# The experts' weights read in neighbouring rows, and the recurrence keys' norms computed in 32-column tiles

## The reference

```python
kk = heads(k * k_k)                      # [L, 8 heads, 64]
kk = kk * lax.rsqrt(jnp.maximum(jnp.sum(kk * kk, axis=-1, keepdims=True), 1e-24))
...
g = jax.nn.sigmoid(hg) @ gate_g2         # [L, 96] @ [96, 512]
```

```python
xs = h[idx]                                               # [128, 1024] per expert
hid = silu(xs @ w_gate[e]) * (xs @ w_up[e])               # w_gate, w_up: [1024, 512]
y = (hid @ w_down[e]) * g                                 # w_down: [512, 1024], added into the output rows
```

## Time and profile before

| | us |
|---|---|
| median of three runs | 4886.32 |
| lowest and highest | 4883.38, 4889.38 |
| the profiled execution | 4879.66 |
| its span on the core | 4877.9 |
| recurrence keys, first scaling to last multiplication | 755.4 to 794.8 |
| experts of layer 0, first to last product of hidden values (L3919) | 3386.6 to 3761.0 |
| experts of layer 1, likewise | 4537.8 to 4821.7 |

### The profile page before, as it was taken

The page is one execution under the profiler, slowest core; times in us unless marked ns, Lnnn a source line. Parts: engine busy times, 40 slices in busy tenths (PEclk is TensorE's granted clock), DMA queues, the critical chain, the costliest instruction groups (busy, mean ns, idle before and its releaser), DMA issues. The chain is left out here.

```text
span 4877.9 us, 89645 instructions
## 1 busy us (share of the span) xinstructions
PE 4396.5 (90%) x39314; PEld 3460.2 (71%) x39314; DVE 2089.0 (43%) x3007; ACT 1367.6 (28%) x2034; POOL 1051.8 (22%) x756
## 2 busy tenths in 40 slices
PE   6998996999998989999989889997999688996897
PEld 3878885999994478888867657674776574774776
DVE  2026544444443134323422144416666414434886
ACT  2114202222222020000012133314665212322775
POOL 2310122444432123333322010021221111000111
PEclk9999997999998999999999889998999889998998
DMA  7310110000006311111121000027998210002998
GB/s 277 100 48 7 44 27 27 4 4 4 3 4 271 116 47 46 49 48 47 47 104 40 26 23 1 14 89 293 301 304 251 83 33 23 1 27 108 337 375 287
DMA packets 322596, 480.33 MB, mean 98 GB/s; under 512 B 43665, under 2 KB 201322, under 8 KB 313042
## 3 DMA queue, kind: packets, MB, share of 16 engines
q1 hardware_dynamic: 301778, 399.61, 23.9%
q0 software_dynamic: 17024, 63.11, 4.6%
q10 hardware_dynamic: 3456, 12.58, 0.7%
HBM read 420.71 MB, written 54.53 MB: 97 GB/s over the span
## 5 line engine op out<-in xcount | busy, mean ns | idle before, releaser
L3895 DVE TENSOR_TENSOR l_experts_lo<-l_raw_room,l_experts_hi 128x1024 fp32r<-128x1024 f32 x256 | 300.2, 1220 | 61.1 <-ACT l_experts_hi L3828 60.6
L3828 ACT ACTIVATE l_experts_hi<-l_raw_room 128x1024 fp32r<-128x1024 f32 x256 | 256.1, 1058 | 66.4 <-PEq L69 32.1
L180 PE MATMUL mlp_ps<-h_hi,mlp_w_hi 128*128 128x512 f32 x512 | 201.0, 393 | 9.0 <-DVE h_lo L590 9.0
L180 PE MATMUL mlp_ps<-h_lo,mlp_w_hi 128*128 128x512 f32 x512 | 200.3, 391 | 0.0
L180 PE MATMUL mlp_ps<-h_hi,mlp_w_lo 128*128 128x512 f32 x512 | 200.2, 391 | 0.0
L1788 POOL TENSOR_TENSOR rec_lv<-rec_ab,rec_masks 128x512 f32<-128x512 f32 x120 | 145.0, 1225 | 243.5 <-DVE rec_ab L1705 157.0
L1724 DVE TENSOR_TENSOR rec_x<-rec_x,rec_all_ps 128x1024 f32<-128x1024 f32 (+1 forms) x100 | 111.4, 1114 | 194.2 <-PE rec_all_ps L1506 194.2
L2369 ACT ACTIVATE mlp_hid_hi<-mlp_pos 128x1024 f32 x32 | 34.0, 1062 | 569.3 <-DVE mlp_pos L2379 569.3
L180 PE MATMUL mlp_ps<-mlp_hid_hi,mlp_w_hi 128*128 128x512 f32 x448 | 174.3, 389 | 0.0
L180 PE MATMUL mlp_ps<-mlp_hid_lo,mlp_w_hi 128*128 128x512 f32 x448 | 174.3, 389 | 0.0
L180 PE MATMUL mlp_ps<-mlp_hid_hi,mlp_w_lo 128*128 128x512 f32 x448 | 174.3, 389 | 0.0
(11 more groups left out here) (716 smaller groups left out, 11507.8 us busy)
## 6 DMA issues: line engine op xcount, KB each, us to landing
l_raw_room<-in_w_gate_dram SPq DMA_DIRECT2D x128, 512.0 KB, 6.6
l_raw_room<-in_w_up_dram SPq DMA_DIRECT2D x128, 512.0 KB, 7.9
l_experts_raw_down<-in_w_down_dram SPq DMA_DIRECT2D x64, 1024.0 KB, 7.5
rec_out_w_ada<-in_w_ada_dram SPq DMA_DIRECT2D x24, 1024.0 KB, 12.3
mlp_w<-in_w_mlp_up_dram SPq DMA_DIRECT2D x32, 512.0 KB, 3.9
mlp_w<-in_w_mlp_down_dram SPq DMA_DIRECT2D x32, 512.0 KB, 4.0
l_choose_w_ada<-in_w_ada_dram POOLq DMA_DIRECT2D x16, 1024.0 KB, 16.6
l_in_w<-in_w_in_dram SPq DMA_DIRECT2D x18, 512.0 KB, 4.1
```

The costliest lines, as they stand in the source:

```text
L180: mm = self.nc.tensor.matmul(ps[0:rows, c, 0:n], w[b][:, k, 0:rows], x[:, k, t0:t0 + n], start=(k + j == 0), stop=(k == kt - 1 and j == 2))
L3828: nc.scalar.activation(hi[:, q % RING], piece(e, u), ACT.Copy).then_inc(hi_done, 1)
L3895: nc.vector.tensor_tensor(lo[:, q % RING], piece(e, u), hi[:, q % RING].bitcast(F32), ALU.subtract).then_inc(lo_done, 1)
```

## The change

Three edits.

1. **Loads.** Gate, up and down are read as `(p k) f`: partition p gets the contraction rows 8p to 8p+7 (gate and up) or 4p to 4p+3 (down). A piece of two steps is thus two neighbouring rows: 4 KB in a row in DRAM for gate and up, 8 KB for down, where before it was two runs of 2 KB or of 4 KB. In SBUF the rows lie as before: gate and up of a partition in two runs of 2 KB with the other matrix between them, down in one run of 8 KB.
2. **Transposes.** So that tokens and hidden values meet these rows, the transposes take every eighth column of `xs` and every fourth of `hid`, where they took 128 neighbouring ones; and the small-token matmuls of gate and up (L3758) take every fourth column of the weights as moving operand. Their numbers and sizes are as before.
3. **Keys.** The sums of squares use a stationary `pick` of 32 columns and move the squares, a quarter of a unit to each column tile of 32: 48 matmuls of 128 or 64 columns that accumulate in one PSUM tile of 128x128. The inverse norms are spread by 48 matmuls with a stationary tile `couples` (made by four DVE copies), each with 32 partitions, into four PSUM banks a unit, two units deep where it was three. Gate products 0 and 1 come after unit 2 of the sums, 2 and 3 between the sums and the spreading. `gout` has room for all four.

```diff
-        pick = s.sb("pick", [P, 2])
-        sq, rs = s.sb("sq", [P, 3, 512]), s.sb("rs", [P, 4 * TT, 2])
+        pick, couples = s.sb("pick", [P, 66]), s.sb("couples", [P, N, P])
+        sq, rs = s.sb("sq", [P, 3, 512]), s.sb("rs", [P, P])
...
+                    if q in (5, 8):
+                        copy_gate(q // 3 - 1)
                 act.wait_ge(clamped, 1)
                 nc.scalar.activation(rs[:], rs[:], ACT.Sqrt).then_inc(rooted, 1)
+                copy_gate(2)
+                copy_gate(3)
...
-                    for c in range(n // P):
-                        mm = nc.tensor.matmul(ss[:, first[q] + c], sq[:, q % 3, c * P:(c + 1) * P], pick[:],
-                                              start=True, stop=True)
+                    for c in QUARTERS:
+                        mm = nc.tensor.matmul(ss[32 * c:32 * c + 32, 0:w], pick[:, 32 - 2 * q:64 - 2 * q],
+                                              sq[:, q % 3, c * w:(c + 1) * w], start=(q == 0), stop=(q == N - 1),
+                                              tile_position=(0, 32 * c))
...
+                gate(2)
+                gate(3)
+                pe.wait_ge(coupled, 4)
                 pe.wait_ge(inv_done, 1)
...
+                    if q == 1:
+                        pe.wait_ge(g_copied, 4)
+                    if q >= 2:
+                        pe.wait_ge(keys_done, q - 1)
+                    for c in QUARTERS:
+                        rows = slice(32 * c, 32 * c + 32)
+                        mm = nc.tensor.matmul(bc[:, q % 2, c, 0:w], couples[rows, q], rs[rows, 0:w], start=True,
+                                              stop=True)
...
-                         w[e].rearrange("(k p) f -> p k f", p=P)[:, 2 * c:2 * c + 2]).then_inc(self.full[c], 16)
+                         w[e].rearrange("(p k) f -> p k f", p=P)[:, 2 * c:2 * c + 2]).then_inc(self.full[c], 16)
...
-                        sp.dma_start(raw_down[:, f // 2], w_down[e].rearrange("(k p) f -> p k f", p=P)[:, f:f + 2]
+                        sp.dma_start(raw_down[:, f // 2], w_down[e].rearrange("(p k) f -> p k f", p=P)[:, f:f + 2]
...
-                                                     xs[0][:, e % 2, (4 * g + k) * P:(4 * g + k + 1) * P], ident)
+                                                     xs[0][:, e % 2, 4 * g + k::KT], ident)
...
-                                piece(e, k).rearrange("p (a f) -> p a f", a=2)[:, :, j * P:(j + 1) * P],
+                                piece(e, k).rearrange("p (a f) -> p a f", a=2)[:, :, j::FT],
...
-                        tr = nc.tensor.transpose(pH[:, f * P:(f + 1) * P], hid[:, f * P:(f + 1) * P], ident)
+                        tr = nc.tensor.transpose(pH[:, f * P:(f + 1) * P], hid[:, f:FE:FT], ident)
```

More of the change, by code:

```diff
@@ L1320, in _ @@
                     sp.wait_ge(g_copied, m + 1)
-                    sp.dma_start(g_dram[m * P:(m + 1) * P, :], gout[:, m % 2]).then_inc(g_stored[m % 2], 16)
-                for b in range(2):
-                    sp.wait_ge(g_stored[b], 32)
+                    sp.dma_start(g_dram[m * P:(m + 1) * P, :], gout[:, m]).then_inc(g_stored, 16)
+                sp.wait_ge(g_stored, 64)
             @block.scalar
@@ L1329, in _, with copy_gate @@
                 nc.scalar.activation(lora_in[0:32, :], lora_a[0:32, :], ACT.Tanh)
+                def copy_gate(m):
+                    act.wait_ge(g_done, m + 1)
+                    nc.scalar.activation(gout[:, m], pg[:, m % 2].rearrange("p c t -> p (c t)"), ACT.Copy
+                                         ).then_inc(g_copied, 1)
                 for q, (m, t0, n) in enumerate(units):
@@ L1360, in _ @@
                     mm.then_inc(summed, 1)
[L1361 to L1364, removed]
-                pe.wait_ge(inv_done, 1)
[L1366 to L1373, removed]
+                    if q == 2:
+                        pe.wait_ge(loaded, 32)
+                        pe.wait_ge(g_ready, 1)
+                        gate(0)
+                        gate(1)
@@ new lines, in _ @@
+                gate(2)
+                gate(3)
+                pe.wait_ge(coupled, 4)
+                pe.wait_ge(inv_done, 1)
+                for q, (_, _, n) in enumerate(units):
+                    w = n // 4
+                    if q == 1:
[6 more added lines that the diff above has]
+                                              stop=True)
@@ L1374, in _ @@
                     mm.then_inc(spread, 1)
[L1375 to L1376 removed]
             @block.vector
             def _(dve):
+                nc.vector.memset(pick[:], 0.0).then_inc(cleared, 1)
+                dve.wait_ge(cleared, 1)
                 for j in range(2):
[L1381 to L1382 removed]
+                    last = nc.vector.memset(pick[64 * j:64 * j + 64, 32 + j:33 + j], 1.0)
@@ L1389, in _ @@
                 nc.vector.memset(lora_in[64:65, :], 1.0)
-                dve.wait_ge(summed, len(units))
-                nc.vector.tensor_scalar(rs[:], ss[:], 1e-24, None, ALU.max).then_inc(clamped, 1)
+                for c in QUARTERS:
+                    rows = slice(32 * c, 32 * c + 32)
+                    nc.vector.tensor_copy(couples[rows].rearrange("p a (h i) -> p (a h) i", h=2),
+                                          ident[rows, 32 * c:32 * c + 2 * N].unsqueeze(2).to_broadcast([32, 2 * N, 64])
+                                          ).then_inc(coupled, 1)
+                dve.wait_ge(summed, N)
+                nc.vector.tensor_scalar(rs[:], ss, 1e-24, None, ALU.max).then_inc(clamped, 1)
                 dve.wait_ge(rooted, 1)
```

31 lines of the change are left out of this document (14 added, 17 removed).

## The result

The changed kernel takes 4932.22 us (median of four runs, 4930.77 to 4940.76), the kernel before 4887.85 beside it on the same chip. The ratio is 1.0096, 95% interval 1.0078 to 1.0113: slower by 38 to 55 us, where 15 us faster was forecast. The profiled execution took 4931.6 us, 51.9 more than that of before. The keys' stage saved what it should; the experts of layer 0 lost nearly six times as much.

What follows compares the result with a forecast made beforehand. Keys' stage bound by a chain, layer 0 by PE, layer 1 by PE, then DMA. Keys -12, down -3, layer 0 and strides 0: 4886.3 - 15 = 4871 us; range 4856 to 4936, forecast alone 4866 to 4877.

Steps and rivals of the forecast that it cites:

- Keys, -12: Keys' stage: sums done at about 770.0, last multiplication at 783 instead of 794.8, saving 12 us, 9 to 14 by the ends.
- Rival 3: Keys' stage keeps its chain: gates before sums at half clock, short units' gaps add 2 to 3; saved 5, 4878, chance 0.08.
- nothing, PE hides it: Loads in layer 0's experts: faster loads gain nothing, since PE is busy for 100.00 of 100 us.
- upper bound of 3.9 us an expert: Layer 0's two small-token groups, moving operand stepping 16 bytes: each element taking twice as long, 62 us over 16 experts.
- I take no cost: Strided reads by PE in small-token matmuls and transposes: 0 us, as float32r columns had shown twice the affected matmuls' rate.
- The second ground: Small-token matmuls: the four column tiles read the same 16 bytes at a time, one float each, supporting no stride cost.
- 39 us was the upper bound: Layer 0's transposes, stationary operand stepping 32 or 16 bytes: at most 2.4 us an expert, 39 us over 16.
- rival 2: Strided elements cost PE time in layer 0: stationary 4910 (0.07), moving 4933 (0.11), both 4972 (0.09); chance 0.27.
- Down, -3: Layer 1 down loads: 512 packets of 4 KB become 256 of 8 KB, 0.2 us an expert over 15 experts, 3 us.
- Gate and up keep 2 KB packets: Gate and up loads: the shorter run, 2 KB in SBUF, sets the packet despite doubled DRAM runs; no gain.
- Rival 1: Layer 1 gate and up do move in 4 KB packets, saving 14 us more: 4857, chance 0.15.
- Layer 1's transposes: no cost: Layer 1's two larger strided transposes: at most 1.75 us an expert, just inside PE's 1.8 us of room.

## Why the prediction was wrong

- **Keys, -12: right, but two of its parts missed and made up for each other.** The stage fell from 39.4 to 27.0 us. It starts 2.5 us earlier than before, so 2.5 are added here to compare with the forecast's clock. The sums ended at 769.4, where 770.0 stood. The second pair of gate products ran wholly at the clock of 1.00, in 3.70 us, and was through at 773.0, where 774.0 to 776.3 were given. The multiplications then took 8.9 us where 7 were taken: DVE is busy for 6.9 of them, and 1.9 are gaps behind the two-deep spreading, 1.2 of it in the stretch where the clock is back at 0.50. The end, 782.4, so met the 783 forecast in part by luck. Rival 3 as a whole did not come, but its gaps nearly did.
- **Layer 0, "nothing, PE hides it": right of the loads, wrong of PE.** The forecast named layer 0 as the place where each microsecond counts sixteen times, and the two groups of 1.93 us as what would be hit, with an upper bound of 3.9 us an expert. The measured cost is 3.9 us an expert (3.8 in the steady periods), the bound itself.
- **The step that failed is "I take no cost" for the strided reads.** Its ground was that the port takes a float32r matmul's columns at twice the rate of the affected ones, so that it had slack. But that rate was shown for neighbouring floats only. (The 0.50 us of plain float32 was a little long, too: from one record to the next the attention scores show 0.43.) Bytes are not what a stride uses up: at a step of 4 floats each 16 bytes hold one float that is wanted, and the group runs at half pace. In float32r, where the slack was measured, any stride loses just that factor of two. The second ground, that the four column tiles read the same 16 bytes at a time, has no support: the whole array pays the same factor. The value was taken from the end that was the cheaper one, not from a row near the case; the forecast itself said that there was none.
- **The rule that spoke against it.** The group went from 1.93 to 2.02 us at step 2, and to 2.92, 3.83 and 3.89 at steps 3, 4 and 8. The Trainium skill, "Advanced Engine Details and Errata", section "Memory Cachelines", says that at least two accesses must hit a 16-byte line to absorb its latency, and that the tolerance depends on the type. In plain float32 the runs agree: with two floats a line, at step 2, next to nothing is lost. In float32r two floats a line are not enough (0.23 to 0.45 us).
- **Stationary side: 39 us was the upper bound, 8 the measured cost.** A load with a stride takes 1.4 to 1.5 times as long, not the whole transpose twice as long, and mostly beside other work. Of rival 2's cases it was the one with both sides that came, which had a chance of 0.09 and a price of 4972: the moving side whole, the stationary one at a fifth. Its price for the moving side alone, 4933, meets the 4932 measured partly by chance. For the profiled execution it means 4879.7 - 15 + 62 = 4926.7, and 4931.6 was measured: layer 0 cost 8.7 more than 62 (1.5 + 65.7 + 3.5), nearly all of it the stationary side; down brought 2.4 less; the keys gave 0.4 more, and stages that the change does not touch gave back 5.8 (2.5 ahead of the keys, 3.3 behind layer 1). The median then lay 0.6 above the profiled execution, not 6.6. That 4932 lies inside the range up to 4936 is due to this rival; the forecast's own range ended at 4877.
- **Down, -3: not seen.** The changed kernel's layer 1 gained 0.6 us. The working took 0.2 us for 15 experts, but rows 10 and 11 show nine periods that DMA bounds, which is 1.8. Layer 1 took between 282.9 and 284.2 us in seven kernels with either packet size for down and 2 KB for gate and up, so what is left can't be told from nothing.
- **Gate and up keep 2 KB packets: right**, and the reason as well: only when both sides had 4 KB did the packets grow. Rival 1's price of 14 us had the same fault as down's; in the kernel that has such packets it was 7.
- **Layer 1's transposes: no cost, as forecast, but not for the reason given.** They were to fit into the 1.8 us that PE has free where DMA bounds. They cost nothing where PE bounds either: with the strided transposes alone, the gate activations from the second to the fifth follow one another at 17.8 us as before, because the two groups of transposes take 1.04 and 0.63 us there for 1.03 and 0.60.

Without the strided operands the edits would be worth 12 us, and 19 with the room ordered for it.

## What to carry to other kernels

A change of a load's layout is paid for by whoever reads the data next: list the operands that turn from neighbouring to strided, and ask for each whether its engine has a gap there. If it has none and no row shows such a read, take the price of the worst case, times the number of passes, before the gain. A DMA's packet is as long as the shorter of its two runs, and longer packets pay only in the periods that DMA bounds; count those in the trace.

## What the runs showed of the hardware

- Moving operand in plain float32, small-token matmuls: 50.2, 52.6, 77.7, 102.5 and 104.4 ns a record of 256 columns in four column tiles at steps of 1, 2, 3, 4 and 8 floats. A step of 2 was all but free; beyond 4 next to nothing was added. In the whole array, 512 columns: 0.43 us at step 1, 0.45 at 2, 0.90 at 4.
- Moving operand in float32r: 0.23 us a matmul of 512 columns at step 1, 0.45 at 2 and 3, 0.46 at 4, 0.43 at 8. Columns read twice over cost next to nothing extra.
- Stationary operand, steps of 4 and 8 floats: 138 to 140 ns a load become 191 to 212.
- Packets in layer 1: 87 ns at 2 KB, 164 at 4 KB (162 with all of gate and up in 4 KB), 315 at 8 KB, 2 KB packets remaining 2 KB when only the DRAM side is made longer.
